# Sublayer changes of a decoder trunk: last unit, norm, update and the next two units by whole tiles of 520 tokens, or by halves of 260

## The reference

```
def rms_norm(x, g):
    xf = x.astype(jnp.float32)
    y = xf * lax.rsqrt(jnp.mean(xf * xf, axis=-1, keepdims=True) + EPS)
    return (y * g.astype(jnp.float32)).astype(x.dtype)
...
        x = x + rms_norm(m, p['post_mix_g'][layer])
        h = rms_norm(x, p['pre_ffn_g'][layer])
        f, cs = conv_ffn(h, conv_prev[layer], p['w_up'][layer], p['conv_w'][layer],
                         p['conv_b'][layer], p['w_down'][layer])
        conv_new.append(cs)
        x = x + rms_norm(f, p['post_ffn_g'][layer])
```

## Time and profile before

| what | value |
|---|---|
| median of three runs | 1606.84 us |
| the profiled execution's own time | 1606.73 us |
| its span, first to last instruction | 1604.8 us |
| TensorE matmul busy | 1474.8 us, 92% |
| DVE, ACT, POOL busy | 907.0 (57%), 555.6 (35%), 208.7 us (13%) |
| mean granted TensorE clock | 0.960 of full |
| chain that ended last | 86% on TensorE, 6% DVE, 3% ACT |
| mean DMA rate | 86 GB/s |

### The profile page before, as it was taken

One profiled execution on the slowest core, in us unless ns is written; L12 is line 12 of the kernel. 1 busy time (PEld: TensorE's weight loads), 2 busy tenths in 40 slices (PEclk: granted clock), 3 DMA queues, 4 the chain that ended last, 5 costly groups with the idle time before them and its releaser, 6 DMA issues.

```text
span 1604.8 us, 29667 instructions
## 1 busy us (share of the span) xinstructions
PE 1474.8 (92%) x11365; PEld 1365.8 (85%) x11365; DVE 907.0 (57%) x1500; ACT 555.6 (35%) x856; POOL 208.7 (13%) x347
## 2 busy tenths in 40 slices
PE   3898899997899999999779999999968999999996
PEld 2798899996799999999779865544958999999995
DVE  2433466225788888633465543255367888885333
ACT  2533544224422222333453232234343222223333
POOL 1000000001223222200010020100022222221000
PEclk9899999998999999999899999779999999999998
DMA  6222122231233332233334163100212333322321
GB/s 207 59 79 79 53 78 66 81 92 52 66 92 91 91 91 85 76 92 91 95 104 172 67 263 119 43 0 1 69 37 79 91 91 91 91 80 87 93 88 53
DMA packets 223097, 138.04 MB, mean 86 GB/s; under 512 B 12508, under 2 KB 218386, under 8 KB 221992
## 3 DMA queue, kind: packets, MB, share of 16 engines
q1 hardware_dynamic: 214432, 110.53, 23.5%
q0 software_dynamic: 4224, 24.62, 4.0%
q10 hardware_dynamic: 4376, 2.00, 0.5%
HBM read 133.82 MB, written 3.67 MB: 86 GB/s over the span
## 4 chain that ended last, share of the span: by engine, by line
PE 86%; DVE 6%; ACT 3%; issue 1%; ACTq 0%; DVEq 0%
PE psum L551 70%; PE psum L847 2%; PE psum L934 2%; DVE x L1443 2%; PE psum L999 2%; DVE ut L1440 2%; PE psum L998 1%; PE psum L1016 1%; PE psum L859 1%; PE psum L874 1%; DVE xl L1428 1%; PE psum L671 1%; PE psum L1008 1%; ACT wh L1061 1%; ACT L1076 1%
## 5 line engine op out<-in xcount | busy, mean ns | idle before, releaser
L551 PE MATMUL psum<-xh,wh 128*128 128x260 f32 x2112 | 435.2, 288 | 48.9 <-DVE xl L1428 33.8
L1407 DVE TENSOR_TENSOR wl<-ws,wh 128x1024 fp32r<-128x1024 f32 x221 | 270.6, 1225 | 366.0 <-ACT wh L1061 363.8
L551 PE MATMUL psum<-xh,wl 128*128 128x260 f32 x2112 | 430.4, 286 | 0.0
L551 PE MATMUL psum<-xl,wh 128*128 128x260 f32 x2112 | 430.3, 286 | 0.0
L1061 ACT ACTIVATE wh<-ws 128x1024 fp32r<-128x1024 f32 x221 | 233.4, 1057 | 529.3 <-PE psum L551 529.2
L551 PEld LDWEIGHTS psum<-xh,wh 128*128 128x128 f32 x2112 | 331.8, 192 | 53.9 <-issue 33.5
L551 PEld LDWEIGHTS psum<-xh,wl 128*128 128x128 f32 x2112 | 330.9, 191 | 0.0
L551 PEld LDWEIGHTS psum<-xl,wh 128*128 128x128 f32 x2112 | 330.9, 192 | 0.0
L551 PE MATMUL psum<-acth,wh 128*128 128x260 f32 x704 | 142.3, 283 | 0.0
L551 PE MATMUL psum<-acth,wl 128*128 128x260 f32 x704 | 141.6, 282 | 0.0
L551 PE MATMUL psum<-actl,wh 128*128 128x260 f32 x704 | 141.3, 282 | 0.0
(11 more groups left out here) (241 smaller groups left out, 1804.3 us busy)
## 6 DMA issues: line engine op xcount, KB each, us to landing
ws<-in_w_up SPq DMA_DIRECT2D x88, 512.0 KB, 3.8
ws<-in_w_in_a SPq DMA_DIRECT2D x32, 512.0 KB, 4.1
ws<-in_w_down SPq DMA_DIRECT2D x32, 384.0 KB, 3.4
ws<-in_w_down SPq DMA_DIRECT2D x32, 320.0 KB, 3.1
ws<-in_w_out_a SPq DMA_DIRECT2D x16, 512.0 KB, 4.1
ws<-in_w_o SPq DMA_DIRECT2D x8, 512.0 KB, 4.6
xn<-in_x_prompt SPq DMA_DIRECT2D x4, 512.0 KB, 10.3
ws<-in_w_dq SPq DMA_DIRECT2D x4, 512.0 KB, 3.9
```

The source lines that it names most:

```text
L551: mm = pe.matmul(psum[:, 2 * slot + b, 0:HB], w, r[:, k, b * HB:(b + 1) * HB], start=st, stop=en)
L1407: dve.tensor_tensor(wl[:, slot2, :], ws[:, slot4, :], f32(wh[:, slot2, :]), ALU.subtract).then_inc(w_low, 1)
```

## The change

Five things, at the four changes:

1. **Halves.** The last weight unit of a sublayer runs all its blocks for tokens 0 to 259, then all for 260 to 519 (`last_unit`), with the sums of squares of each half beside it (`half_rms`). Norm, update, high and low parts and the next two units then go half by half (`update` of ACT and DVE, `locked_units`). The output is transposed and written by halves, in 8 DMAs of 256 KB and 2 for the samples.
2. **Gain in the copy.** ACT's copy of a sublayer output is scaled by the gain, so that DVE can multiply and add two tiles in one instruction (only the first two tiles of the first half go singly).
3. **Squares of x on TensorE.** POOL's additions go. ACT squares two half tiles at once, TensorE multiplies each by ones (`sum_pair`, 2 matmuls a pair).
4. **One table set.** `roots()` loads a table set that holds Ln and Exp, ahead of the wait for the sum.
5. **Third weight slot.** The second unit of each pair has `wh` and `wl` of its own (over unused parts of the arena), so both units of a pair are converted before the last unit ends, and the third unit is converted during the update. The third unit also goes to PSUM slot 2 (banks 4 and 5), so it waits for no evacuation. Unit four is converted in the tile behind.

```diff
+LOCKED = [U_UP[0], U_KV, U_UP[1]]
+THIRD = [n + 1 for n in LOCKED]
+def slot_free(n):
+    if n in THIRD:
+        return 0
+    if any(n in (m + 2, m + 3) for m in LOCKED):
+        return n - 2
+    return n - 1
...
+            def last_unit(n, ks, rh, rl, first, name, koff=0):
+                pe.wait_ge(w_low, n + 1)
+                for kk, k in enumerate(ks):
+                    mm = product(n, 1, weight_slot(n), k, koff + kk, rh, rl, first and kk == 0, kk == len(ks) - 1, parts=(0,))
+                mm.then_inc(part_done, 1)
+                for kk, k in enumerate(ks):
+                    mm = product(n, 1, weight_slot(n), k, koff + kk, rh, rl, first and kk == 0, kk == len(ks) - 1, parts=(1,))
+                    if kk == 2:
+                        half_rms(name, 0)
+                mm.then_inc(mm_done, 1)
+                half_rms(name, 1)
+            def half_rms(name, h):
+                if h == 0:
+                    pe.wait_ge(sq_added, SQA[name] + KD - 2)
+                    wait(pe, ln_done, SSB[name])
+                pe.matmul(psum[:, 6 + h, 0:HB], ones[:, :], sqa[:, HALF[h]], start=True, stop=False)
+                pe.wait_ge(sq_done, SQB[name] + KD + h)
+                pe.matmul(psum[:, 6 + h, 0:HB], ones[:, :], sq[:, 1, HALF[h]], start=False, stop=True).then_inc(ss_done, 1)
+            def locked_units(n, rh, rl, sem, base, m_name, x_name):
+                pe.wait_ge(w_low, n + 2)
+                for h in range(2):
+                    pe.wait_ge(m_ready, MB[m_name] + KD + h)
+                    for t in range(KD):
+                        pe.wait_ge(sem, base + KD * h + t + 1)
+                        for e in range(2):
+                            mm = product(n + e, e, weight_slot(n + e), t, t, rh, rl, t == 0, t == KD - 1, parts=(h,))
...
+                        if t % 2:
+                            sum_pair(x_name, h, t // 2)
...
             def rms(name, dst):
-                act.activation(warm[:, :], ones[:, 0:1], ACT.Ln)
...
+            def roots():
+                act.preload_act_table_set("natural_log_exp_and_others")
...
+            def update(p, name, m):
+                gain = POST[p] + KD - 1
+                sq_slot_free(name, KD - 1)
+                for h in range(2):
+                    if h:
+                        act.wait_ge(mm_done, (U_UP[0], U_KV, U_UP[1], U_END)[p - 1])
                     else:
+                        act.wait_ge(part_done, p)
+                    act.activation(sq[:, 1, HALF[h]], psum[:, 2 + h, 0:HB], ACT.Square).then_inc(sq_done, 1)
+                    if h == 0:
+                        roots()
+                        rms(name, r2, 0)
+                    act.activation(m[:, KD - 1, HALF[h]], psum[:, 2 + h, 0:HB], ACT.Copy, scale=pt[:, gain:gain + 1]).then_inc(m_ready, 1)
...
+                        for t in (2 * g, 2 * g + 1):
+                            act.wait_ge(x_new, 2 * KD * (p - 1) + KD * h + t + 1)
+                            act.activation(dst[:, t, HALF[h]], x[:, t, HALF[h]], ACT.Copy, scale=pt[:, gains + t:gains + t + 1]).then_inc(done, 1)
...
+                            act.wait_ge(sq_summed, 6 * (p - 1) + i - 1 - (i > 5))
+                        act.activation(halves(sq[:, i % 2, :]), x[:, 2 * g:2 * g + 2, HALF[h]], ACT.Square).then_inc(sq_done, 1)
+                        if i == 0:
+                            rms(name, r2, 1)
+                        elif i == 2:
+                            ahead_static(LOCKED[p - 1])
+                        elif i == 5:
+                            rms(f"x{p}", r1, 0)
+                rms(f"x{p}", r1, 1)
...
+                for h in range(2):
+                    dve.wait_ge(r_ready, SSB[name] + h + 1)
+                    if h and p < 4:
+                        ahead_static(LOCKED[p - 1])
+                    for g in range(4):
+                        for t, n in ((0, 1), (1, 1)) if h == g == 0 else ((2 * g, 2),):
...
-                for t in range(KD):
-                    add_squares(pool, f"x{1 + 2 * l}", t, t % 2)
```

More of the change, by code:

```diff
@@ L545, in _, with product @@
         def _(pe):
-            def product(n, slot, nslot, k, kk, rh, rl, first, last):
-                hw, lw = wh[:, nslot, kk * P:(kk + 1) * P], wl[:, nslot, kk * P:(kk + 1) * P]
+            def product(n, slot, nslot, k, kk, rh, rl, first, last, parts=(0, 1)):
+                if nslot == 2:
+                    hw, lw = (w[:, kk * P:(kk + 1) * P] for w in weights(n))
+                else:
+                    hw, lw = wh[:, nslot, kk * P:(kk + 1) * P], wl[:, nslot, kk * P:(kk + 1) * P]
                 for w, r, st, en in ((hw, rh, first, False), (hw, rl, False, False), (lw, rh, False, last)):
-                    for b in range(2):
+                    for b in parts:
                         mm = pe.matmul(psum[:, 2 * slot + b, 0:HB], w, r[:, k, b * HB:(b + 1) * HB], start=st, stop=en)
@@ L1112, in raw @@
+            def raw(name, t, slot, m_dst, gain):
                 square(acc(slot), name, t, slot % 2)
                 fixed_wait()
-                act.activation(halves(m_dst), acc(slot), ACT.Copy).then_inc(m_ready, 1)
+                scale = pt[:, gain + t:gain + t + 1] if isinstance(t, int) else pt[:, bass.ds(gain + t, 1)]
+                act.activation(halves(m_dst), acc(slot), ACT.Copy, scale=scale).then_inc(m_ready, 1)
             for k, (src, r0, b, lo, n) in enumerate(PACK):
@@ L1237, in down @@
                     t = 2 * i + e
-                    last = isinstance(t, int) and t == KD - 1
-                    for w in range(3 if last else 4):
+                    for w in range(4):
                         if guard:
@@ L1434, in update @@
+            def update(p, name, m):
                 if p % 2 == 0:
                     dve.wait_ge(csn_sent, 16 * 9 * (p // 2))
-                for t in range(KD):
-                    k = KD * (p - 1) + t
-                    wait(dve, x_new, k - 1)
-                    dve.scalar_tensor_tensor(out=ut[:, t % 2, :], in0=m[:, t, :], scalar=pt[:, POST[p] + t:POST[p] + t + 1], in1=r2[:, :],
-                                             op0=ALU.mult, op1=ALU.mult).then_inc(u_mul, 1)
-                    dve.wait_ge(u_mul, k + 1)
-                    dve.tensor_tensor(x[:, t, :], x[:, t, :], ut[:, t % 2, :], ALU.add).then_inc(x_new, 1)
-                    if p < 4 and t:
-                        low(p, t - 1)
@@ L1589, in tile @@
                                       ALU.mult).then_inc(evac_up, 1)
-                    ahead(U_UP[l], 4, i, u)
+                    if not first:
+                        ahead(U_UP[l], 4, i, u)
                     if b == 0 and not first:
```

363 lines of the change are left out of this document (207 added, 156 removed).

## The result

Four runs of the changed kernel took 1550.58 to 1556.25 us, median **1553.34**; four of the kernel before took 1606.13 to 1609.2, median 1607.41. The ratio is 0.9662, 95% interval [0.9649, 0.9675]. The forecast was 1551. Five further runs of the changed kernel gave 1551.81, with 1607.06 for the nine runs of the kernel before that were taken beside them. The profiled run is the slowest of its four, 1556.25 us, with a span of 1554.5; against the 1606.73 of the profiled run before that is 50.5 us less, against the medians 54.1.

What follows compares the result with a forecast made beforehand. TensorE's matmuls bound the kernel (92% busy, 86% of the chain); the change shortens breaks. Savings of 15.8 + 14.4 + 16.7 + 6.0 + 2.7 = 55.6 us from 1606.73 gave 1551; own range 1546 to 1556, 8 in 10 1544 to 1566.

Steps and rivals of the forecast that it cites:

- DVE's start: At each change of sublayer, DVE starts 0.2 to 1.4 us after E, the last unit's end without the sum inside it.
- The pair: Two units after a change: TensorE paces at 2.31 us per two half tiles, last sum 22.8 us after DVE's start.
- the 0.7 us "lost" there: At the pair's turn between halves, DVE first makes `wl` of the third unit and 0.7 us is lost.
- The fourth unit: First change: TensorE waits 1.3 us for its weights; it starts 29.8 us after DVE's start.
- The clock: Rival, 0.16: TensorE's clock falls to half in the gap before the pair; 7 us over three changes, 1558.
- The case I leaned on: In the old trace TensorE's clock stayed full after 1.97 us idle; in the other near case, 2.18 us, it fell.
- In-order waits: Rival, 0.12: ACT's square waits for TensorE's sum, with copies queued behind; 0.4 us a turn, 10 us in all, 1561.
- ACT as what DVE waits for in the middle of a half: In the pair: a sign that the forecast is wrong, with no size given.
- the long forms: Rival, 0.03: DVE's slow instructions in the pair aren't POOL's doing; +5 us a change, 1566.
- The set is kept: At the norms, against a rival, 0.05: Ln and Exp go on loading a table each; 19 us back, 1570.
- The end: After `m_ffn1`: last add 4.3 us earlier, 1.7 from the smaller last DMA, together 6.0 us.
- Table loads elsewhere: In the norms of `x0` and `v` the second load goes: 2.7 us with the tiny activation; `kv` and `cq` nothing.

Runs made afterwards that it cites:

- cheap sums: The changed kernel with the sums of squares of x over 8 columns in place of 260: 1547.93 us, ratio 0.9635.

## Why the forecast was right, and where it was off

- **DVE's start.** Forecast E+0.2, +1.4, +0.3, +1.3; measured 0.23, 1.40, 0.24, 1.38. Every piece of the chain square, load, sum, Ln, Exp was as priced, and the load ends 0.2 us before it is needed.
- **The pair.** The sum came out, the path only in part. The low part comes 3.0 us after DVE's start and TensorE at 3.65, for 3.6; pairs every 2.31 to 2.32, ended by TensorE; at full clock 23.0 for 22.8. The price taken for the broadcast multiply, 0.70 between 0.70 and 1.40, was right: 0.69. But TensorE is the pace in the second half alone. In the first the chain runs through DVE up to the turn, and the 0.7 us "lost" there are just what TensorE's slower pace leaves of DVE's; cheap sums left the start of the second half where it was (13.66 us for 13.67).
- **The fourth unit.** The wait for `wl` is 1.66 and 1.71 us for 1.3, and 0.45 after `m_ffn0` for 0.4. Start 30.45 for 29.8 after DVE's start: 0.2 from the pair, 0.05 from the third unit, 0.4 from this stall.
- **The clock** is the step that failed. The forecast left it out of the sum, at 0.16; in both profiles of the changed kernel it fell in two pairs of three, in the first change and after `m_ffn0`. The size was overpriced, 7 us for three falls; the two cost 1.6 and 2.1, 3.7 together, and that is most of what the three changes lack. The case I leaned on, with 1.97 us idle and a full clock, was one of two near the gap, and the other one held.
- **In-order waits** came with the clock. The timeline of the first change:

```profile
380.40 0.64 ACT L1232 ACTIVATE sq<-x 128x520 f32<-128x520 f32 x1 [1.57 <-PE psum L644]
380.94 1.04 ACT L1153 ACTIVATE wh<-ws 128x1024 fp32r<-128x1024 f32 x1
...
382.42 0.89 DVE L1552 SCALAR_TENSOR_TENSOR xl<-x,pt,xh 128x260 fp32r<-128x260 f32 x2 [1.53 <-ACT xh L1224]
```

TensorE's sum, slow at half clock, holds ACT's square up for 1.57 us; a weight's conversion and the copies are queued behind the square, and DVE waits 1.53 us for them in the middle of the half. The chain takes this way from TensorE over ACT to DVE, so it is how the fall cost 1.6 us there. The forecast had named just this, ACT as what DVE waits for in the middle of a half, as a sign of being wrong; it priced clock and queues as two rivals, and here they came as one. After `m_ffn0` DVE waits 2.04 us for ACT in the same place, but there the chain stays on TensorE. In the third change, at full clock, DVE waits nowhere in the pair for over 0.1 us.
- **POOL** was the cause of the long forms: its additions on one column close that rival. That the long and the short forms part exactly by POOL's spans was misread, though: the add at 393.75 runs beside a POOL addition and takes 0.70 us, and the instruction behind it takes 1.78. **The set is kept**: eight loads at the norms in the whole kernel for 22 before.
- **The end.** The last add at E+13.2 for 12.4, mostly since a multiply and its dependent add take 1.42 us and not 1.35; the end at E+18.2 for 17 to 18. The last issue, at 1552.21, is of the small output and is followed by 2.3 us where there were 4.4: a gain of 2.1 for the 1.7 taken from the middle.
- **Table loads elsewhere**: 2.7 us, not separable from the 3 us by which the start varies. That the profiled run has 4.7 there is partly that, and partly luck.
- **The rule on table loads** that I set aside, the Trainium skill ("ScalarE: Activation LUTs", What ACT_TABLE_LOAD costs), would add a drain to each load; the runs with one load less (1.37 us earlier) and one more (1.27 us later) leave no room for it here. By the rule of the Trainium skill on the default of the clock ("TensorE: Matmul & The Clock Gate", What's actually happening) a short gap in dense work might pass; after the attention it did, in the two other changes it did not.
- **The number.** The profiled run lies 5.1 us over the forecast: the changes and the end lack 5.7, the stretches between them 1.6, the start gives 2.0 more than its term, and 0.2 are gained outside the span. That the median is only 2.3 over it comes of the two runs of 1550.6 and 1550.7 us, of which there is no trace; whether they are nearer the forecast by its mechanism or by the draw of the clock and the start isn't known.

## What to carry to other kernels

Measure a break from the end of the last work before it to the first work that must wait for all of it, and price the engine that paces each part of it: removing a cost only pays down to the next engine's pace, here 0.1 us away. Before giving a helper engine work "off the path", look whether the main engine's instructions beside it get longer: here some 19 us came from the neighbours of POOL's additions, not from waits for them. When a rival slows one engine, follow what stands in order behind it on the others: here a slow sum held up a square, and behind the square the copies that DVE needed. Moving work to TensorE and shortening its idle time belong together, because the half clock that follows a long gap is free only while TensorE isn't the pace.

## What the runs showed of the hardware

- A gap of 1.68 us brought the clock to half in the first change and left it at full after the attention, in the same kernel and in both of its profiles. Over the four profiles with these gaps left open the clock fell in the first pair in three, in the second (gap 2.35 us) in four, in the third in none. Before the gaps TensorE was busy; why they differ isn't settled. Filled with 8 small matmuls, 9 pairs of 9 (three profiles) stayed at full.
- 3.4 us at half clock made a pair 1.6 us longer where TensorE's sums were full, and 6 us of it 2.1 us; where the sums were cheap and DVE the pace, 3.4 us cost 0.3.
- A POOL addition of two operands over 520 columns lengthens a DVE instruction that starts while it runs from 0.75 to 1.80 us (or 0.70 to 1.68), all 14 of them in the three old pairs; the four that had started before it keep their length. Of nine DVE adds that start within 0.01 us of a POOL addition five keep their 0.70 and four take 1.84 to 1.86. Cut to one column (0.19 us in most) the additions leave none longer than 0.76.
- The half clock's lost time, one less the granted clock summed over the span, fell from 64 us in the profile before to 43 us in that of the changed kernel. Part of it was hidden before, so it isn't all gain; but shorter breaks also pay in clock.
- The same program's time before the first change varies by 3 us from run to run, more than some of the edits tried here are worth; they could be told apart in the stages of the profile, and hardly in the total.
